# FFN units as one run of 512-column and one of 256-column matmuls, and new byte offsets for the operands of the split

## The reference

```python
def rmsnorm(x, g):
    return x * lax.rsqrt(jnp.mean(x * x, axis=-1, keepdims=True) + EPS) * g

h = h + (jax.nn.silu(a @ w_gate[i]) * (a @ w_up[i])) @ w_down[i]      # first block, D_FF = 2816
h = swiglu(rmsnorm_2(x, norm_ffn1_pre[l]), w_ffn1_in[l], w_ffn1_out[l])   # second block, twice
h = mixer(rmsnorm_2(x, norm_mix_pre[l]), w_mix_in[l], ...)
```

## Time and profile before

| | |
|---|---|
| median of 3 runs | 799.43 us (799.36 to 799.44) |
| profiled execution | 799.74 us, of which the span from first to last instruction is 798.0 us |
| PE busy | 787.5 us, 99% of the span, 4710 matmuls |
| weight loads (PEld) | 693.1 us, 87% |
| DVE busy | 533.2 us, 67% |
| ACT busy | 429.7 us, 54% |
| granted TensorE clock | 1.000 of full speed over the whole span, which is the level of 2.4 GHz |

### The profile page before, as it was taken

How to read it: one execution, slowest core, us unless ns; L and a number is a source line. 1 busy time by engine, 2 the same in 40 slices (tenths; PEclk the granted TensorE clock), 3 DMA queues, 4 the chain that set the end, 5 groups by cost and what they waited for, 6 DMA issues and landing times.

```text
span 798.0 us, 12182 instructions
## 1 busy us (share of the span) xinstructions
PE 787.5 (99%) x4710; PEld 693.1 (87%) x4710; DVE 533.2 (67%) x628; ACT 429.7 (54%) x565; POOL 28.3 (4%) x35
## 2 busy tenths in 40 slices
PE   8999999999999999999999999999999999999997
PEld 8989979888888888888888887999988888888885
DVE  7865567766666667866666566766977766666665
ACT  6556658444544548744544446565557644454444
POOL 0000000000000000000000000002420000000000
PEclk9999999999999999999999999999999999999999
DMA  8633433655555553665545554452444655555531
GB/s 329 236 113 117 142 109 142 225 183 185 208 166 204 184 184 110 241 227 187 207 165 206 182 186 158 143 200 107 159 171 160 223 211 175 193 198 172 208 105 53
DMA packets 20797, 141.16 MB, mean 177 GB/s; under 512 B 2448, under 2 KB 2704, under 8 KB 4384
## 3 DMA queue, kind: packets, MB, share of 16 engines
q1 hardware_dynamic: 20192, 138.65, 48.6%
q0 software_dynamic: 576, 2.10, 0.7%
HBM read 139.69 MB, written 1.05 MB: 176 GB/s over the span
## 4 chain that ended last, share of the span: by engine, by line
PE 94%; ACT 2%; DVE 2%; issue 1%; DMA 1%; SPq 0%; DVEq 0%; ACTq 0%
PE ps L1463 93%; ACT whi L680 1%; DMA raw<-wstream 1%; PE ps L1469 1%; DVE x L1212 0%; ACT squared L695 0%; DVE xa L1019 0%; PE ps L1700 0%; DVE wlo L1008 0%; PE ps L1670 0%; PE ps L1902 0%; DVE xg L1207 0%; DVEq L270 0%; ACT L913 0%; PE ps L1702 0%
## 5 line engine op out<-in xcount | busy, mean ns | idle before, releaser
L1463 PE MATMUL ps<-xa,whi 128*128 128x512 f32 (+2 forms) x1744 | 488.6, 348 | 0.0
L1463 PE MATMUL ps<-xa,wlo 128*128 128x256 f32 (+1 forms) x1376 | 383.0, 281 | 0.0
L1008 DVE TENSOR_TENSOR wlo<-raw,whi 128x2048 fp32r<-128x2048 f32 x128 | 293.7, 2295 | 82.4 <-ACT whi L680 82.3
L1463 PEld LDWEIGHTS ps<-xa,whi 128*128 128x128 f32 x1744 | 302.2, 188 | 44.6 <-issue 2.1
L1463 PEld LDWEIGHTS ps<-xa,wlo 128*128 128x128 f32 x1376 | 258.7, 189 | 1.1
L680 ACT ACTIVATE whi<-raw 128x2048 fp32r<-128x2048 f32 x128 | 244.3, 1910 | 6.9 <-PE ps L1463 6.8
L1463 PE MATMUL ps<-whi,hhi 128*128 128x512 f32 x240 | 93.8, 391 | 0.0
L1463 PE MATMUL ps<-whi,hlo 128*128 128x512 f32 x240 | 93.7, 390 | 0.0
L1463 PE MATMUL ps<-wlo,hhi 128*128 128x512 f32 x240 | 93.5, 390 | 0.0
L874 ACT ACTIVATE hhi<-arena 128x512 fp32r<-128x512 f32 x30 | 19.0, 632 | 88.9 <-PE ps L1463 82.4
L860 ACT ACTIVATE arena<-ps 128x512 f32<-128x512 f32 x33 | 19.7, 596 | 87.5 <-PE ps L1463 87.2
(11 more groups left out here) (221 smaller groups left out, 531.9 us busy)
## 6 DMA issues: line engine op xcount, KB each, us to landing
raw<-wstream SPq DMA_DIRECT2D x128, 1024.0 KB, 4.8
gain_row<-rows_in POOLq DMA_DIRECT2D x4, 512.0 KB, 3.9
x<-x_in SPq DMA_DIRECT2D x2, 512.0 KB, 3.9
raw<-wstream SPq DMA_DIRECT2D x2, 512.0 KB, 5.9
out<-x SPq DMA_DIRECT2D x4, 256.0 KB, 2.0
xg<-const_in SPq DMA_DIRECT2D x1, 912.0 KB, 12.0
small<-small_in SPq DMA_DIRECT2D x1, 152.0 KB, 6.3
arena<-meta_in SPq DMA_DIRECT2D x1, 64.0 KB, 4.6
```

The lines of the kernel that those rows point to most:

```text
L1008: nc.vector.tensor_tensor(wlo[slot][:], raw[slot][:], whi[slot][:].bitcast(F32), ALU.subtract).then_inc(lo_ready, 1)
L1463: return nc.tensor.matmul(o, lhsT, rhs, start=start, stop=stop, skip_group_check=True)
```

## The change

It has two parts.

1. **Order in an FFN unit.** A gate unit first does all 16 matmuls of 512 columns (`hi_products`) and then all 16 of 256 (`lo_products`). An up unit does the 256s first and then the 512s. In both, the block `a` (and with it the PSUM bank) now changes with every matmul, and each bank is still summed over `kt`. A gate unit waits for `hi_ready` ahead of its first half and for `lo_ready` only ahead of its second. In group 1 the two small matmuls that spread the row scale stand in the middle of the gate's 512s. The first unit of an FFN keeps its order.

2. **Places in SBUF.** `ya` is cut into `y_hi` and `y_lo`. The tensors are placed so that `whi`, `xa`, `y_hi` and `hhi` start at residue 128 modulo 512 bytes; after them come 192 unused bytes (`gap`), and `wlo`, `y_lo` and `hlo` start at residue 320. For the FFNs and the mixer `xa` is now addressed through `xn`, a view with rows of 512 float32 (2048 bytes), so that all slices `kt` start at one residue: 128 in the FFNs (and the norm ahead of them), and 448 in the mixer, whose view starts 80 float32 further on. The input projection keeps the row of 544 float32, and thus four residues in turn for `xa`, while its `wlo` moves to 320.

```diff
+XN_AT = (0, 0, 80, 0)
+LOW_GAP = 48
...
         whi = [sb(f"whi{s}", [P, UNIT], F32R) for s in range(SLOTS)]
+        xa = sb("xa", [P, KT, 2 * TOK], F32R)
+        y_hi = sb("y_hi", [P, KT, SEQ], F32R)
+        hhi = sb("hhi", [P, 2, 256], F32R)
+        sb("gap", [P, LOW_GAP])
         wlo = [sb(f"wlo{s}", [P, UNIT], F32R) for s in range(SLOTS)]
-        xa = sb("xa", [P, KT, 2 * TOK], F32R)
-        ya = sb("ya", [P, KT, 2 * SEQ], F32R)
-        hhi = sb("hhi", [P, 2, 256], F32R)
+        y_lo = sb("y_lo", [P, KT, SEQ], F32R)
         hlo = sb("hlo", [P, 2, 256], F32R)
...
+        xa_line = xa[:].rearrange("p k c -> p (k c)")
+        xn = [xa_line[:, c:c + KT * 2 * SEQ].rearrange("p (k c) -> p k c", k=KT) for c in XN_AT]
...
-            def paired_tile(bank, slot, a):
-
-                for kt in range(KT):
-                    w = slice(kt * 256 + a * P, kt * 256 + (a + 1) * P)
-                    mm(ps[:, bank, :], whi[slot][:, w], xa[:, kt, 0:2 * SEQ], kt == 0, False)
-                    ins = mm(ps[:, bank, 0:SEQ], wlo[slot][:, w], xa[:, kt, 0:SEQ], False, kt == KT - 1)
-                return ins
...
-                def two_tiles(unit, slot, bank, spread=False):
-                    pe.wait_ge(lo_ready, unit + 1)
-                    paired_tile(bank, slot, 0)
-                    if spread:
-                        spread_rstd((0, 1, 3)[f], 2)
-                    paired_tile(bank + 1, slot, 1).then_inc(unit_used, 1)
+                norm = (0, 1, 3)[f]
+
+                def hi_products(bank, slot, start, spread=False):
+
+                    for kt in range(KT):
+                        if spread and kt == KT // 2:
+                            spread_rstd(norm, 2)
+                        for a in range(2):
+                            w = slice(kt * 256 + a * P, kt * 256 + (a + 1) * P)
+                            ins = mm(ps[:, bank + a, :], whi[slot][:, w], xn[norm][:, kt, 0:2 * SEQ], start and kt == 0, not start and kt == KT - 1)
+                    return ins
+
+                def lo_products(bank, slot, start):
+
+                    for kt in range(KT):
+                        for a in range(2):
+                            w = slice(kt * 256 + a * P, kt * 256 + (a + 1) * P)
+                            ins = mm(ps[:, bank + a, 0:SEQ], wlo[slot][:, w], xn[norm][:, kt, 0:SEQ], start and kt == 0, not start and kt == KT - 1)
+                    return ins
 
                 def gate(g, unit, slot, first):
                     pe.wait_ge(gate_out, g + base)
-                    two_tiles(unit, slot, 4, first)
+                    pe.wait_ge(hi_ready, unit)
+                    hi_products(4, slot, True, first)
+                    pe.wait_ge(lo_ready, unit + 1)
+                    lo_products(4, slot, False).then_inc(unit_used, 1)
 
                 def up(g, unit, slot):
                     if not isinstance(g, int) or g:
                         pe.wait_ge(up_out, g + base)
-                    two_tiles(unit, slot, 6)
+                    pe.wait_ge(lo_ready, unit + 1)
+                    lo_products(6, slot, True)
+                    hi_products(6, slot, False).then_inc(unit_used, 1)
```

More of the change, by code:

```diff
@@ L873, in hidden_hi @@
                         act.wait_ge(unit_used, down_before + 1)
-                    nc.scalar.activation(ya[:, 0:2, 0:SEQ] if last else hhi[:], hact, ACT.Copy).then_inc(hhi_done, 1)
+                    nc.scalar.activation(y_hi[:, 0:2, :] if last else hhi[:], hact, ACT.Copy).then_inc(hhi_done, 1)
                 split_ahead(unit0)
@@ L1272, in hidden_lo @@
                 def hidden_lo(g, last=False):
-                    hi, lo = (ya[:, 0:2, 0:SEQ], ya[:, 0:2, SEQ:2 * SEQ]) if last else (hhi[:], hlo[:])
+                    hi, lo = (y_hi[:, 0:2, :], y_lo[:, 0:2, :]) if last else (hhi[:], hlo[:])
                     dve.wait_ge(hhi_done, g + (base + 1))
@@ L1513, in first_paired_unit @@
                         w = slice(kt * 256 + a * P, kt * 256 + (a + 1) * P)
-                        mm(ps[:, bank + a, 0:SEQ], whi[slot][:, w], xa[:, kt, 0:SEQ], kt == 0, False)
-                        mm(ps[:, bank + a, 0:SEQ], wlo[slot][:, w], xa[:, kt, 0:SEQ], False, False)
+                        mm(ps[:, bank + a, 0:SEQ], whi[slot][:, w], xn[k][:, kt, 0:SEQ], kt == 0, False)
+                        mm(ps[:, bank + a, 0:SEQ], wlo[slot][:, w], xn[k][:, kt, 0:SEQ], False, False)
                 for kt in range(KT):
@@ L1519, in first_paired_unit @@
                         w = slice(kt * 256 + a * P, kt * 256 + (a + 1) * P)
[L1520 removed]
+                        ins = mm(ps[:, bank + a, SEQ:2 * SEQ], whi[slot][:, w], xn[k][:, kt, SEQ:2 * SEQ], False, kt == KT - 1)
                 return ins
@@ L1534, in first_columns_unit @@
                         w = slice(kt * 256 + c, kt * 256 + c + P)
-                        mm(o, whi[slot][:, w], xa[:, kt, 0:SEQ], kt == 0 and c == 0, False)
-                        mm(o, wlo[slot][:, w], xa[:, kt, 0:SEQ], False, False)
+                        mm(o, whi[slot][:, w], xn[k][:, kt, 0:SEQ], kt == 0 and c == 0, False)
+                        mm(o, wlo[slot][:, w], xn[k][:, kt, 0:SEQ], False, False)
                 for kt in range(KT):
@@ L1540, in first_columns_unit @@
                         w = slice(kt * 256 + c, kt * 256 + c + P)
-                        ins = mm(o, whi[slot][:, w], xa[:, kt, SEQ:2 * SEQ], False, kt == KT - 1)
+                        ins = mm(o, whi[slot][:, w], xn[k][:, kt, SEQ:2 * SEQ], False, kt == KT - 1)
                 return ins
@@ L1548, in tokens_tile @@
                     w = slice(kt * 256, (kt + 1) * 256)
-                    mm(o, xa[:, kt, hi], whi[slot][:, w], kt == 0, False)
-                    mm(o, xa[:, kt, hi], wlo[slot][:, w], False, False)
-                    ins = mm(o, xa[:, kt, lo], whi[slot][:, w], False, kt == KT - 1)
+                    mm(o, xn[2][:, kt, hi], whi[slot][:, w], kt == 0, False)
+                    mm(o, xn[2][:, kt, hi], wlo[slot][:, w], False, False)
+                    ins = mm(o, xn[2][:, kt, lo], whi[slot][:, w], False, kt == KT - 1)
                 return ins
@@ L1824, in ffn @@
                 pe.wait_ge(hlo_done, base + GROUPS)
-                rows_last_unit(n % SLOTS, [(ya[:, a, 0:SEQ], ya[:, a, SEQ:2 * SEQ]) for a in range(2)], (1, 2, 4)[f])
+                rows_last_unit(n % SLOTS, [(y_hi[:, a, :], y_lo[:, a, :]) for a in range(2)], (1, 2, 4)[f])
             ffn(0)
@@ L1922, in _ @@
                     pe.wait_ge(lo_ready, n + 1)
-                    parts = [(ya[:, m, 0:SEQ], ya[:, m, SEQ:2 * SEQ]) for m in MIXOUT_ORDER[2 * i:2 * i + 2]]
+                    parts = [(y_hi[:, m, :], y_lo[:, m, :]) for m in MIXOUT_ORDER[2 * i:2 * i + 2]]
                     if i == N_OUT - 1:
```

33 lines of the change are left out of this document (16 added, 17 removed).

## The result

The changed kernel takes 800.85 us in the median of 20 runs, against 799.43 us before in 20 runs; the ratio is 1.0018 with a 95% interval of [1.0012, 1.0024]. It is slower by 1.4 us, where 5.4 us less were forecast. The time lies inside the range given (786.0 to 801.5), and the difference is just under the 0.2% that was counted as one; the sign was wrong.

A forecast was written before the change was run, and what follows sets the result against it. PE, busy 99% of the span, was taken as the bound, through its matmul steps. Terms of -4.2, -0.4 and -0.8 us summed to -5.4, so a median of 794.0 us, range 786.0 to 801.5.

The forecast's parts named there:

- What bounds the kernel: Whole kernel: PE, busy 99% of 798.0 us, sets the time through steps between matmul starts; its waits are 4.8 us.
- the rival that nothing moves: Whole kernel: a fixed toll of 14 ns per matmul whatever its neighbours leaves 799.4 us; chance 0.13.
- The 512s of a unit in a run: Gate and up pairs: 512s at 226.7 ns and 256s at 117.4 make 344.1 instead of 348.3, -4.2 us.
- the start of a run: Down units' nine slow first 512s: the slow head moves to up or goes; -0.4 us, kept 0 to -1.2.
- The 256s: Gate and up: each 256 in a run of 32 costs 117.4 ns; the uncertain term, with break-even at 121.6 ns.
- The low bound of 113.3: Gate and up: a 256 at 113.3 ns, from one pair of 0.34 us, would make this part -8.4 us.
- Mixer and first units: Mixer and FFNs' first units: 720 matmuls with one activation residue go from 119.0 to 117.9 ns, -0.8 us.
- The sign named for it: Mixer: seven kt of a block must come from 2.50 to 2.48 us if the 1.1 ns holds.
- Down units and output projections: 984 matmuls of 512 columns: streamed weights jump between residues 128 and 320, but pairings are kept, so 0.
- the case that the jump counts: Down and output matmuls: if the jump counted as the alternation does, 227 would go to 231 ns, +4.1 us.
- the sign of being wrong: FFN units in the later profile: 32 256s over 3.89 us, or a down unit over 5.5 us.
- The rival of the broken pace: Down, output, FFN pairs and mixer: jumps to low parts break the pace; +8.9 us, 808.3 in full; chance 0.19.

The follow-up runs named there:

- `xa` at 448: The changed kernel without the 192 unused bytes, with the FFNs' `xa` slices at residue 448 instead of 128: 793.91 us, ratio 0.9929 against the kernel before.

## Why the prediction was wrong

**What bounds the kernel: right.** The whole difference sits in steps between PE's starts, and no wait appeared.

**Where the number fell.** 800.85 us lies where the rival that nothing moves had put it (797.9 to 801.0), but not by its mechanism: -2.6 and +3.95 us nearly cancel.

**The 512s of a unit in a run: mechanism right, size half.** -4.2 us was forecast for gate and up, -1.88 was measured (0.2 of the 4.2 came from a pair put at 348.3 ns, where its own rows give 348.1). The settled step of 226.7 came as read from the down unit, but it needs constant residues as well as the run (the order alone showed 231), and a run does not start with it. The 16 of gate take 0.02 us more than 16 x 226.7 and the 16 of up 0.05 more: 0.07 x 30 = 2.1 us. The step that failed is the one on the start of a run: I had seen the nine slow 512s at the head of the down unit, and allowed for their moving to up, but put half of their going into the sum (-0.4) and took 226.7 for all the 512s of gate and up. The steps show heads in both: gate begins with four steps of 232 ns on average, as down now ends out of pace, and up with nine such steps, as 256s end there.

**The 256s: right in number, by luck.** 117.4 was taken from the earlier trace rows and 117.5 measured. But the earlier trace rows average a run over four residues in turn, and the new run has one distance of 64 in the slower of its two paces. The same order costs 120 without the gap and 113.4 with `xa` at 448. The low bound of 113.3 was real as well: it came with another layout, and in two up units of the changed kernel itself.

**Mixer and first units: right in size.** -0.8 forecast, -0.68 + 0.08 = -0.60 measured. The sign named for it was 2.48 us for seven kt of a block; the block of the earlier trace rows came to 2.45 (512.06 to 514.51 us), while the first units lost a little.

**Down units and output projections: the step that failed first, and turned the sign.** I put 984 matmuls at 0 because streamed and loaded operands stay equal in pairs, and kept +4.1 us for the case that the jump counts. The runs show that it counts: +3.15 + 0.16 + 0.48 + 0.16 = +3.95 us, and the sign of being wrong, a down unit over 5.5 us, came with 5.58. The rule that I used, that equal pairs suffice, had no row behind it; the earlier trace rows showed 226.7 only where nothing moved at all. What the earlier trace rows showed, a step that changes with the residue of one operand, spoke for the bound, and I had given that case 0.19. The rival of the broken pace is what happened in its first half, without its second: the rows lost 4.0 us, and the 256s lost nothing. It had set its point of decision at 3.1 to 5.5 ns a row with the full gain elsewhere; with half the gain elsewhere the 4.0 ns measured were enough.

**The rule of the skill.** The Trainium skill (TensorE: Matmul & The Clock Gate, section "Step-by-step: what each phase is for") says that loading the next weights takes nothing from the running matmul. Moving only the streamed operand's address changed 16 dense 512-column matmuls from 3.62 to 3.74 us here, and moving stream and load together by 192 bytes changed nothing (3.68 both times). So the two are not independent at this scale, and the measurement decides.

## What to carry to other kernels

Where PE is never idle, the few ns of each matmul beyond its columns are still there to win: keep streamed and loaded operands at constant addresses modulo 256 bytes through a run of matmuls, measure a few distances and take the best, and do not let one operand jump to please another stage. Price an address change in every stage that reads the tensor, and test order and placement together, since here the order alone gave nothing, the placement alone cost 6.2 us, and the same order on another placement gained 5.7 us. When reading a settled step from a trace, read the unsettled head of the run too, and count how many runs the change makes.

## What the runs showed of the hardware

- The step of dense float32r matmuls repeats when the streamed operand moves by 256 bytes: 3.62 and 3.63 us for 16 of 512 columns, 3.83 and 3.83 for 32 of 256 (`xa` at 128 and 384), and again the same at 192 and 448.
- With the five distances tried, a 256-column matmul of the loop costs 113 to 120 ns and a 512-column one 226.7 to 234, for 106.7 and 213.3 ns of columns. The best of them is 64 for the 256s and 0 for the 512s.
- Runs of like matmuls at like addresses (distance 64) went at 113 to 114 or at about 117.7 ns to their end: the mixer's first unit between kernels, the up units within the changed kernel.
- In the traces at distance 0 a 512-column run takes three to ten steps of 231 to 233 ns on average before it settles at 226.7: nine after alternation and nine after the 256s of the changed kernel's up unit. It has no such head where 512s that had settled stand ahead of it, as in the down unit without the gap.
- Alternating each operand of the down unit between two residues 192 bytes apart costs 0.14 us in 24 matmuls (5.58 against 5.44), with stream and load at one residue throughout.

What inside the chip makes this period and these paces was not found.
